# Scores of the first unit and its choice of experts pulled into the query phase, gathers issued before its end, and score matmuls of half height

## The reference, cut to what matters

```python
def _peer(tok, wq, subkeys, u_tab, v_tab):      # 16384 experts, 8 heads, 128 keys a half, 16 chosen
    def chunk(hc):                               # 128 tokens
        q = (hc @ wq).reshape(PEER_CHUNK, PEER_HEADS, 2, PEER_DK // 2)
        s = jnp.einsum('chpd,hpnd->chpn', q, subkeys, preferred_element_type=jnp.float32)
        s1, i1 = lax.top_k(s[:, :, 0], PEER_TOPK)
        s2, i2 = lax.top_k(s[:, :, 1], PEER_TOPK)
        cand = (s1[..., :, None] + s2[..., None, :]).reshape(PEER_CHUNK, PEER_HEADS, PEER_TOPK * PEER_TOPK)
        sc, ic = lax.top_k(cand, PEER_TOPK)
        e = (jnp.take_along_axis(i1, ic // PEER_TOPK, axis=-1) * PEER_NKEYS
             + jnp.take_along_axis(i2, ic % PEER_TOPK, axis=-1))
        g = jax.nn.softmax(sc, axis=-1)
        a = jax.nn.gelu(jnp.einsum('chkd,cd->chk', u_tab[e], hc, preferred_element_type=jnp.float32),
                        approximate=False)
        return jnp.einsum('chk,chkd->cd', (g * a).astype(v_tab.dtype), v_tab[e])
```

## Time and profile before

| | |
|---|---|
| median of 3 runs | 5551.96 us (5547.89 to 5558.19) |
| the profiled execution | 5560.93 us, span 5559.0 us |
| busy share of the span | TensorE 68%, VectorE 60%, ScalarE 36%, GpSimd 36% |
| queue of the gathers | 1342.26 MB of 1521.85 MB in all, 59.1% of the 16 DMA engines' span |
| gathers (L466) | 1280, 1137 ns each on GpSimd, 11.7 us from issue to landing in the median |
| the dots (L637) | 1280, 1272 ns each |

### The profile page before, as it was taken

One profiled execution on the slowest core, in us unless ns is written; L12 is line 12 of the kernel. 1 busy time (PEld: TensorE's weight loads), 2 busy tenths in 40 slices (PEclk: granted clock), 3 DMA queues, 4 the chain that ended last, 5 costly groups with the idle time before them and its releaser, 6 DMA issues. The chain is left out here.

```text
span 5559.0 us, 59850 instructions
## 1 busy us (share of the span) xinstructions
PE 3805.2 (68%) x19548; PEld 1872.1 (34%) x19548; DVE 3349.7 (60%) x7118; ACT 2002.9 (36%) x5166; POOL 2014.7 (36%) x1537
## 2 busy tenths in 40 slices
PE   6899879977555555555567767688976555555554
PEld 3686348866111111111122234356853111111111
DVE  6623451232777777777677777654134777777776
ACT  5422012222343343434344344405223434343343
POOL 4121002221444444444474345401423444444443
PEclk8999989988777777777778889889978777776777
DMA  5011001111999999999998989811216999999998
GB/s 232 16 50 61 4 27 63 63 46 38 421 419 411 416 412 417 416 415 413 368 360 357 361 340 358 322 50 37 98 52 247 419 410 420 410 414 415 412 416 344
DMA packets 228372, 1521.85 MB, mean 274 GB/s; under 512 B 25876, under 2 KB 26260, under 8 KB 56028
## 3 DMA queue, kind: packets, MB, share of 16 engines
q0 software_dynamic: 184320, 1342.26, 59.1%
q1 hardware_dynamic: 43740, 175.77, 8.5%
HBM read 1506.92 MB, written 11.01 MB: 273 GB/s over the span
## 5 line engine op out<-in xcount | busy, mean ns | idle before, releaser
L518 PE MATMUL psum<-arena 64*64 64x512 f32 x10240 | 1769.7, 825 | 1288.6 <-ACT arena L497 1286.2
L466 POOL DMA_INDIRECT arena<-in_uv,arena x1280 | 1455.5, 1137 | 1756.6 <-PE psum L518 1373.2
L637 DVE SCALAR_TENSOR_TENSOR arena<-arena 128x1024 f32<-128x1024 f32 x1280 | 1628.4, 1272 | 747.7 <-DMA arena<-in_uv,arena 720.5
L518 PEld LDWEIGHTS psum<-arena 64*64 64x64 f32 x10240 | 418.0, 169 | 2583.2 <-ACT arena L497 1988.7
L1503 PE MATMUL psum<-view_at,view_at 128*128 128x512 f32 (+1 forms) x4896 | 968.0, 359 | 22.3 <-PEq L164 12.6
L263 POOL TENSOR_TENSOR view_at<-view_at,view_at 128x1024 fp32r<-128x1024 f32 (+1 forms) x196 | 455.0, 2331 | 1407.2 <-ACT view_at L297 1364.7
L486 ACT ACTIVATE arena<-arena 128x1 f32<-128x1 f32 x1280 | 258.2, 202 | 1864.9 <-DVE arena L637 1860.1
L1503 PEld LDWEIGHTS psum<-view_at,view_at 128*128 128x128 f32 x4896 | 814.6, 191 | 195.9 <-issue 65.6
L497 ACT ACTIVATE arena<-arena 128x64 f32<-128x64 f32 x1280 | 445.1, 348 | 55.2 <-PE psum L518 13.3
L490 ACT ACTIVATE arena<-arena 128x1 f32<-128x1 f32 x1280 | 376.8, 294 | 46.7 <-ACT arena L486 0.4
L297 ACT ACTIVATE view_at<-view_at 128x1024 fp32r<-128x1024 f32 (+1 forms) x176 | 163.3, 938 | 322.4 <-DMA view_at<-in_w_in 182.3
(11 more groups left out here) (239 smaller groups left out, 3617.9 us busy)
## 6 DMA issues: line engine op xcount, KB each, us to landing
view_at<-in_w_in SPq DMA_DIRECT2D x108, 512.0 KB, 5.9
view_at<-in_w_mod SPq DMA_DIRECT2D x48, 1024.0 KB, 9.6
arena<-in_uv,arena POOLq DMA_INDIRECT x1280, 11.7
view_at<-in_w_br SPq DMA_DIRECT2D x48, 256.0 KB, 2.6
view_at<-in_w_out SPq DMA_DIRECT2D x16, 512.0 KB, 7.9
view_at<-in_wq SPq DMA_DIRECT2D x16, 512.0 KB, 5.1
keep_spectrum<-arena SPq DMA_DIRECT2D x18, 256.0 KB, 7.5
arena<-in_dft SPq DMA_DIRECT2D x1, 4096.0 KB
```

Of the source, the lines that this page charges most:

```text
L466: nc.gpsimd.indirect_dma_start(out=self.slots[i % self.ring], out_offset=None, in_=self.table, in_offset=bass.IndirectOffsetOnAxis(ap=self ...
L518: last = nc.tensor.matmul(self.c.psum[tokens, at:at + 512], self.diag[rows, k % 4], self.slots[k % self.ring][rows, D + h * 512:D + (h + 1 ...
L637: nc.vector.scalar_tensor_tensor(out=self.junk, in0=self.slots[i % self.ring][:, 0:D], scalar=1.0, in1=self.h2_turned if i % 2 else self.h ...
```

## The change

Five things change, in both layers.

1. The query is kept in eight separate places (`qTs`), clear of the first seven slots and of what the early `topk` writes.
2. Scores are made in groups of four units. Each unit is two matmuls of half height, 64x128 stationary and 64x128 moving, one on partitions 0 to 63 and one on 64 to 127, into two PSUM banks. ScalarE copies a group at once, 128x1024. Two groups fit into PSUM.
3. Group 0 (tile 0, heads 0 to 3) is made between the fifth and the sixth projection, behind a wait for the keys.
4. VectorE runs `topk` of unit 0 in the query phase as soon as group 0 is kept. ScalarE makes its exponential after the last projection is kept and before group 1 is copied.
5. GpSimd does the iota and the first seven gathers at the end of its list, behind its wait for the last projection. The `Experts` object is made before the query phase, which now ends without the drain.

```diff
+    EARLY = 4
+
+    def start_vector(self, dve):
+        self.c.nc.vector.tensor_tensor(self.ident2, ...).then_inc(self.ident2_made, 1)
+        later = self.cand, self.cand_cut, self.hot1, self.hot2
+        self.cand, self.cand_cut, self.hot1, self.hot2 = (self.c.at(124 + i, TOPK, TOPK) for i in range(4))
+        for _ in self.topk(dve, 0):
+            pass
+        self.cand, self.cand_cut, self.hot1, self.hot2 = later
+
+    def start_scalar(self, act):
+        self.softmax_exp(act, 0)
+
+    def start_gpsimd(self, pool):
+        self.gather(pool, self.EARLY)
...
-            if i == 0:
-                softmax_exp(0)
...
-            if i == 0:
-                nc.vector.tensor_tensor(self.ident2, ...).then_inc(self.ident2_made, 1)
-                for _ in self.topk(dve, 0):
-                    pass
...
-def phase_query(c, layer, full):
+def phase_query(c, layer, full, experts):
-    qT = c.at(104, PH, T_ALL)
+    qTs = [c.at(at, T_ALL) for at in (104, 107, 110, 113, 116, 194, 197, 200)]
-    with Phase(nc) as ph:
+    GROUP = 4
+    groups = len(units) // GROUP
+    with Phase(nc, gathers=True) as ph:
...
+        def scores_at(g):
+            return c.psum[:, 2048 + (g % 2) * 1024:2048 + (g % 2 + 1) * 1024].rearrange("p (b u n) -> p b u n", b=2, u=GROUP)
...
             pool.wait_ge(proj, PH)
             nc.gpsimd.memset(scores[:, len(units)], 0.0).then_inc(pad, 1)
+            experts.start_gpsimd(pool)
...
+            def score(g):
+                if g >= 2:
+                    pe.wait_ge(score_kept, g - 1)
+                for u in range(g * GROUP, (g + 1) * GROUP):
+                    t, h = units[u]
+                    for half, rows in enumerate((TOP, BOTTOM)):
+                        last = nc.tensor.matmul(scores_at(g)[:, half, u % GROUP], qTs[h][rows, t * P:(t + 1) * P],
+                                                keys[rows, h, half * NK:(half + 1) * NK], start=True, stop=True)
+                last.then_inc(scored, 1)
...
+                if h == GROUP:
+                    pe.wait_ge(keys_in, 16)
+                    pe.wait_ge(kept, GROUP)
+                    score(0)
             pe.wait_ge(kept, PH)
-            for u, (t, h) in enumerate(units):
-                if u >= 8:
-                    pe.wait_ge(score_kept, u // 2 - 3)
-                at = 2048 + (u % 8) * 256
-                nc.tensor.matmul(c.psum[:, at:at + 256], qT[:, h, t * P:(t + 1) * P], keys[:, h, :],
-                                 start=True, stop=True).then_inc(scored, 1)
+            for g in range(1, groups):
+                score(g)
...
+                if h == GROUP:
+                    keep(0)
+            experts.start_scalar(act)
+            for g in range(1, groups):
+                keep(g)
...
+        @ph.block.vector
+        def _(dve):
+            dve.wait_ge(score_kept, 1)
+            experts.start_vector(dve)
```

More of the change, by code:

```diff
@@ L448, in free, with softmax_exp @@
         self.c.nc.all_engine_barrier(sem_only=True)
+    EARLY = 4
+    def start_vector(self, dve):
+        self.c.nc.vector.tensor_tensor(self.ident2, self.c.ident[:, 0:HD], self.c.ident[:, HD:P], ALU.add).then_inc(self.ident2_made, 1)
+        later = self.cand, self.cand_cut, self.hot1, self.hot2
[7 more added lines that the diff above has]
+        self.gather(pool, self.EARLY)
+    def softmax_exp(self, act, u):
+        act.wait_ge(self.exp_ready, u + 1)
+        self.c.nc.scalar.activation(self.exps[:, u % 2], self.topc, ACT.Exp, bias=self.small[:, u % 2, 0:1],
+                                    accum_out=self.small[:, u % 2, 1:2]).then_inc(self.exp_done, 1)
     def up_to(self, n, ahead):
@@ L473, in weigh @@
         nc = self.c.nc
[L475 to L478, removed]
         for i in range(self.n_weighed, self.up_to(n, -1)):
@@ L499, in weigh @@
             if k == 12 and u + 1 < self.units:
-                softmax_exp(u + 1)
+                self.softmax_exp(act, u + 1)
             self.n_weighed = i + 1
@@ L625, in dot @@
             u, k = divmod(i, TOPK)
-            if i == 0:
-                nc.vector.tensor_tensor(self.ident2, self.c.ident[:, 0:HD], self.c.ident[:, HD:P], ALU.add).then_inc(self.ident2_made, 1)
-                for _ in self.topk(dve, 0):
-                    pass
             if i % self.per_tile == 0:
@@ L2544, in _, with keep @@
                 feature_job(c, ring.parts(h), 1024 * (h % 2), width, KD, (h2_high, c.hT_low)).then_inc(proj, 1)
-            pe.wait_ge(keys_in, 16)
+                if h == GROUP:
+                    pe.wait_ge(keys_in, 16)
+                    pe.wait_ge(kept, GROUP)
+                    score(0)
             pe.wait_ge(kept, PH)
-            for u, (t, h) in enumerate(units):
-                if u >= 8:
-                    pe.wait_ge(score_kept, u // 2 - 3)
-                at = 2048 + (u % 8) * 256
-                nc.tensor.matmul(c.psum[:, at:at + 256], qT[:, h, t * P:(t + 1) * P], keys[:, h, :],
-                                 start=True, stop=True).then_inc(scored, 1)
+            for g in range(1, groups):
+                score(g)
         @ph.block.scalar
         def _(act):
+            def keep(g):
+                act.wait_ge(scored, g + 1)
+                nc.scalar.activation(scores[:, g * GROUP:(g + 1) * GROUP].rearrange("p u (b n) -> p b u n", b=2), scores_at(g),
+                                     ACT.Copy).then_inc(score_kept, 1)
             ring.round_ahead(act, -1, proj)
@@ L2559, in _ @@
                 act.wait_ge(proj, h + 1)
-                nc.scalar.activation(qT[:, h, 0:width], c.psum[:, (h % 2) * 1024:(h % 2) * 1024 + width],
+                nc.scalar.activation(qTs[h][:, 0:width], c.psum[:, (h % 2) * 1024:(h % 2) * 1024 + width],
                                      ACT.Copy).then_inc(kept, 1)
[L2562 to L2566, removed]
+                if h == GROUP:
[7 more added lines that the diff above has]
+            experts.start_vector(dve)
 def phase_experts(c, experts, last):
@@ L2667, in build @@
         phase_norm2(c, 0, True)
-        phase_query(c, 0, True)
         experts = Experts(c, 0, range(NT), (4, 0, 4, 0, 4, 4))
+        phase_query(c, 0, True, experts)
         latents = NT_LAT * experts.per_tile + 8
@@ L2678, in build @@
         phase_norm2(c, 1, False)
-        phase_query(c, 1, False)
         experts = Experts(c, 1, range(NT_LAT), (0, 4, 0, 4))
+        phase_query(c, 1, False, experts)
         phase_experts(c, experts, experts.n_all)
```

## The result

The kernel after takes 5520.01 us, the median of 5 runs (5512.13 to 5524.18), beside 5551.07 of the kernel before (5547.54 to 5558.19, 5 runs). The ratio is 0.9938, with a 95% interval of 0.9925 to 0.9951: 34 us faster (27 to 42). The forecast was 50.5 us, 5501.5 us for the time. The range of 5490 to 5524 holds the time; the sum's own bounds, 5494 to 5510, do not.

What follows compares the result with a forecast made beforehand. The DMA-bound stream of gathers was taken as the limit, so its start counts: 29.3 - 0.3 (layer 0) + 21.5 (layer 1) = 50.5 us off the median of 5551.96 gives 5501.5 us; range 5490 to 5524.

Steps and rivals of the forecast that it cites:

- the sum's own bounds: Whole kernel: 1 us either way per layer for projections, 0 to 2 for the stream, 4 for the run: 5494 to 5510.
- The limit is the stream of gathers, and its start counts: Both layers' expert stages: DMA-bound gathers, so an earlier first gather saves its lead, 29.3 us in layer 0, 21.5 in layer 1.
- the rivals: Whole kernel: consumers' lead only (0.09), halves not overlapping (0.07), slower stream (0.10), first gather held to the phase's end (0.04).
- Group 0 between the projections: Query phase: scores between fifth and sixth projections delay their end by 1.2 us in layer 0, 1.8 in layer 1.
- The iota holds half of topk: Query phase: topk's second half waits for the iota behind the last projection; layer 0's first gather at 1352.5, 29.3 us earlier.
- the signs: Profile after: expected marks, such as layer 0's first gather about 5.7 us after the last projection's end (4.5 to 7).
- if the iota cost nothing: Query phase: without the iota's cost, the first gather's lead would be 3.4 us more.
- The scores and their copies: Query phase: group 1.0 us, copy pace 1.1; layer 0's 11 copies take 12.1 us, next phase starts at 1363.5.
- the halves of a unit don't overlap: Rival, scores: group 1.74 us, layer 0's phase ends 7 us later, gain 43 us, 5509 us; chance 0.07.
- Do the slots come free in time?: Start of experts: consumers free slots just in time for the ninth gather; 0.3 us taken off, bounds 0 and 2.
- The margin of half a microsecond: Layer 0, ninth gather: lands at 1379.1, the stream would bring it at 1379.6, so the stream just doesn't run dry.
- only the consumers' lead counts: Rival, both layers: late slots starve the stream; lead falls to 18.3 + 12.2 = 30.5 us, 5521.5 us; chance 0.09.

Runs made afterwards that it cites:

- e10: The changed kernel unchanged, run once more on the chip of e9; 5498.34 us, ratio 0.9893 to the kernel before.
- e11: The kernel before itself, run once more with nothing changed; 5551.23 us, ratio 1.0003.
- the first profile: Unless said to be of the kernel before: the changed kernel's profile from the result, before the follow-up runs; median 5520.01 us, ratio 0.9938.
- e1: The changed kernel unchanged, run again; 5505.80 us, ratio 0.9923 to the kernel before.
- e3: Against the changed kernel, the iota is GpSimd's first instruction in the query phase, no longer in the gather code; 5507.45 us, ratio 0.9919 to the kernel before.
- e5: Against the changed kernel, GpSimd makes only the iota in the query phase, the first gather waits for the next phase; 5515.64 us, ratio 0.9941 to the kernel before.
- e6: Against the kernel before, only the scores changed: half height, groups of four behind the last projection, nothing early; 5538.81 us, ratio 0.9980.
- e7: Against e5, SyncE loads seven contiguous 1 MiB blocks into the slots by ordinary DMAs from the last projection on; one execution, 5536.85 us.
- e2: Against the changed kernel, scores are full-height matmuls again, still in groups of four; 5503.94 us, ratio 0.9925 to the kernel before.
- e8: Against e4, only groups 0 to 4 are half height, later ones full height; 5505.35 us, ratio 0.9917 to the kernel before.
- e12: e4 run once more, beside the kernel before; 5499.96 us, ratio 0.9907.
- e9: Against e8, 16 filler matmuls on TensorE ahead of the first sum of each layer; 5497.11 us, ratio 0.9893 to the kernel before.
- e4: Against the changed kernel, groups of scores rotate over four places in PSUM instead of two; 5503.43 us, ratio 0.9918 to the kernel before.

## Why the prediction came out as it did

**The limit is the stream of gathers, and its start counts.** Right. The sum assumed groups on time, so the pair that fits it is e10 and e11, both without a late sum and from one chip; it was picked after their traces were seen. The timelines of e11, for layer 0's memset and 520th dot, and of both for the last dot of layer 1:

```profile
1349.82 0.31 POOL L2536 MEMSET arena<- 128x256 f32 x1 [26.22 <-PE psum L1503]
...
2707.35 1.23 DVE L637 SCALAR_TENSOR_TENSOR arena<-arena 128x1024 f32<-128x1024 f32 x1
...
4188.12 0.31 POOL L2536 MEMSET arena<- 128x256 f32 x1 [14.82 <-PE psum L1503]
...
5517.17 1.23 DVE L637 SCALAR_TENSOR_TENSOR arena<-arena 128x1024 f32<-128x1024 f32 x1 [1.19 <-DMA arena<-in_uv,arena]
```

```profile
4168.05 0.31 POOL L2554 MEMSET arena<- 128x256 f32 x1 [16.76 <-PE psum L1515]
...
5473.71 1.23 DVE L649 SCALAR_TENSOR_TENSOR arena<-arena 128x1024 f32<-128x1024 f32 x1 [1.23 <-DMA arena<-in_uv,arena]
```

Layer 0: 2707.35 - 1349.82 = 1357.5 against 2677.55 - 1349.63 = 1327.9, less 1.1 for the longer projections: 28.5 us (forecast 29.0). Layer 1: 1329.05 against 1305.66, less 2.4: 21.0 (forecast 21.5). Together **49.5 us against 50.5**. That it fits to 1 us is in part luck: with the first profile of the kernel before in e11's place the same sum gives 52, and by the runs e10 is 59 us (50 to 68) ahead. Of the first profile against e11 it gives 1357.5 - 1336.1 - 1.1 = 20.3 and 1329.1 - 1308.4 - 4.1 = 16.6, together 36.9, within the 27 to 42 us of the result. Of the 12.6 us between the two sums 1.7 are longer projections in layer 1 and the other 10.9 lie behind the memsets, where the groups were late.

So the mechanism was right, and the forecast of 5501.5 was not met in the result, by 18.5 us. The time lies in the range because the range took in the rivals and the spread of the runs.

**Group 0 between the projections.** Right in layer 0: the projections from the first on grew by 1.1 us, those from the fifth on by 1.3 (1.2 forecast). The keys made TensorE wait in layer 1 only, as forecast. There the size was off: the projections grew by 2.4 us in e10, 4.1 in the first profile and 6.2 in e1, for 1.8. TensorE's wait for the keys was 0.9, 1.6 and 2.2 of that, for 0.6.

**The iota holds half of topk.** Right, to 0.1 us: 4.4 us from memset to first gather, forecast 4.5. (The 5.7 us among the signs counts from where the projections ended in the kernel before.) That the wait is worth 3.4 us "if the iota cost nothing" was wrong: e3 took it away and gained nothing, since the ninth gather didn't move. e3 had late groups. With groups on time it was not run; e10's margin of 0.2 us, worked out at the end, leaves little to gain there either.

**The scores and their copies.** This step failed in the first profile and in e1. It took a group at 1.0 us and a pace of 1.1. In e5, e6, e7, e10 that holds (1.14), and a group by itself took 0.89 us, its 16 weight loads with it. In the first profile and e1 groups 4 to 7 came 0.9 to 4.4 us late, by the trace's times of the semaphore that ScalarE waits for. Behind that the granted clock fell to 0.5, the lower level of 1.2 GHz; by its records TensorE had been idle for 2.9 of the 5 us before. The next groups came 1.7 us apart. The phase ended 7 us late. The rival "the halves of a unit don't overlap" has the same 7 us, by another cause: here the halves overlapped, and the lateness came from outside. None of the rivals names it.

**Do the slots come free in time?** The margin of half a microsecond was the right thing to name. The chain gave 25.0 us for the ninth gather, and e10 has 25.1 and no pause. With 7 us on top of it the DMA engines stood still for 4.1 us, and moved less before and behind that. The windows from 24 to 40 us after the memset, the first profile and e10:

```profile
1375.20:1391.20 16.00, 9.73 (x60) 2.82 (x64) 14.45 (x39) 6.76 (x24) 6.16 (x6) 0.71 0.63 225
```

```profile
1373.60:1389.60 16.00, 9.80 (x64) 2.50 (x60) 14.27 (x41) 5.07 (x18) 9.48 (x8) 0.71 1.00 409
```

That is 225 GB/s for 409, so (409 - 225) x 16/415 = 7 us of the stream are lost, nearly all of the 8.2 us by which the 520th dot is later. In layer 1 the ninth gather was forecast 23.4 us after the memset and came at 22.7 in e10 and 26.5 in the first profile, without a full stop of the stream. The rival "only the consumers' lead counts" thus came about in part in layer 0 of the first profile and e1: a lead of 20 to 21 us, between the 29 of the stream and the 11 left to the consumers.

**What the late groups need.** Three things together, each by a run that lacks it: half height (full height beside gathers was on time in e2 and e8, whose sums were late), gathers beside the scores (e5 and e7), and an execution, or a chip, where sums complete late as well (e10, e12). Which of the two it is, why, and what half height does to be open to it, stays open; so does whether GpSimd's issuing or the gathers' transfers do it. e7 and e5 were not run together with a half-height kernel with gathers, so that such a kernel would have shown late groups on that occasion is inferred from their 70-odd late sums.

**The spread.** The stretches between, which the change doesn't touch, differ by 10 us and more between profiles (854.6 to 868.9 us for dots 519 to 767). Much of the difference between ratios of one kernel comes from there.

No version is clearly faster than the changed kernel. e12 and e9 are as fast as e10, within what can be told.

## What to carry to other kernels

When a long run of transfers is the limit, find the first wait that can starve it: here the ninth gather, eight slots behind the first. (When the first gather goes much earlier still, as in e3, an earlier one can starve it: the eighth, which waits for the next phase.) Moving the first transfer earlier is worth something only as long as the consumers free its slot in time, so give both chains the same head start and work out the margin between them. Where that margin is under a microsecond, name the step ahead of it whose price was never measured beside the transfers; here it was the half-height matmul. And profiles of both kernels from the same chip, and alike in whether sums complete late, are needed before a few microseconds are put down to the change.

## What the hardware showed that was not expected

Pairs of matmuls on different halves of the array ran at 0.89 us for 16 records, and their weight loads overlapped. But beside seven indirect gathers they were late by up to 4.4 us in four traces, by the semaphore. The granted clock was still 1.0 when it began: in the first profile the first late copy came 6.5 us after the memset, and the clock fell at 12.7. Beside 420 GB/s of ordinary loads (e7) they weren't late, and full-height ones beside gathers weren't either (e2, e8). In two traces of the same kernels, with the same gathers, on a chip other than that of e1, e3 and e4, they weren't late at all.

In e11 the first gather landed 6.2 us after its issue, the second 3.5 later, and from there one each 2.5; the ninth landed 27.0 us after the first issue. As an estimate from that, a ring of eight slots forgives 27.0 - 6.2, some 20.9 us from the first issue to the ninth. e10 needed 20.7 (1374.77 - 1354.04) and had no pause. e9 needed 22.2 and had none either, but its stream went down to 324 GB/s for 8 us. The first profile needed 27.5 (1383.07 - 1355.58) and had a pause of 4.1.
